# New states of the sample sequences: products over 32 rows, two sequences in different rows in turn, with four banks claimed at once

## The reference, cut to what matters

```python
s = (jnp.exp(b_last)[..., None] * s
     + jnp.einsum('bjhd,bjhv->bhdv', kc * jnp.exp(b_last[:, None] - b), vc))
```

## Time and profile before

| what | value |
|---|---|
| median of 3 runs | 1321.51 us |
| the profiled execution's own time | 1328.91 us |
| its span | 1327.0 us |
| TensorE busy | 1269.0 us (96%) |
| VectorE, ScalarE busy | 437.7 us (33%), 230.6 us (17%) |
| moved by DMA | 454.19 MB, mean 342 GB/s |
| mean granted TensorE clock | 0.983 of 2.4 GHz |

### The profile page before, as it was taken

The page is one execution under the profiler, slowest core; times in us unless marked ns, Lnnn a source line. Parts: engine busy times, 40 slices in busy tenths (PEclk is TensorE's granted clock), DMA queues, the critical chain, the costliest instruction groups (busy, mean ns, idle before and its releaser), DMA issues.

```text
span 1327.0 us, 16958 instructions
## 1 busy us (share of the span) xinstructions
PE 1269.0 (96%) x6497; PEld 702.9 (53%) x6497; DVE 437.7 (33%) x871; ACT 230.6 (17%) x360; POOL 29.3 (2%) x43
## 2 busy tenths in 40 slices
PE   6999999999899999999999999999999999999993
PEld 6999999987543434343443434343443434343431
DVE  4665565654322241313132231313132231313135
ACT  4633334410101011011101011011101011011112
POOL 0000010200000000000000000000000000000002
PEclk9999999999789999999999999999999999999997
DMA  9524444673589999999999999999999999999981
GB/s 379 193 106 143 162 155 157 262 292 127 198 332 377 418 416 417 417 418 417 417 417 416 416 418 418 417 418 417 417 417 416 417 416 418 417 418 417 417 337 41
DMA packets 81366, 454.19 MB, mean 342 GB/s; under 512 B 7437, under 2 KB 7565, under 8 KB 44456
## 3 DMA queue, kind: packets, MB, share of 16 engines
q1 hardware_dynamic: 77264, 439.63, 82.0%
q0 software_dynamic: 4064, 14.03, 3.1%
HBM read 447.44 MB, written 6.31 MB: 342 GB/s over the span
## 4 chain that ended last, share of the span: by engine, by line
PE 92%; DVE 4%; issue 2%; DMA 1%; ACT 0%; DVEq 0%; SPq 0%; ACTq 0%
PE bank L919 33%; PE bank L942 17%; PE bank L649 13%; PE bank L898 10%; PE bank L963 4%; PE bank L717 3%; PE bank L692 2%; PE bank L928 1%; PE bank L931 1%; PE bank L774 1%; PE bank L857 1%; DVE arena L1610 1%; DVE arena L1597 1%; PE bank L906 1%; PE bank L741 1%
## 5 line engine op out<-in xcount | busy, mean ns | idle before, releaser
L919 PE MATMUL bank<-ring,arena 128*64 128x512 f32 x1536 | 349.6, 595 | 0.0
L919 PEld LDWEIGHTS bank<-ring,arena 128*64 128x64 f32 x1536 | 119.5, 137 | 205.8 <-issue 205.8
L649 PE MATMUL bank<-arena_r,ring_r 128*128 128x320 f32 x848 | 182.8, 316 | 0.0
L942 PE MATMUL bank<-ring,arena 128*64 128x512 f32 x768 | 169.3, 593 | 1.3 <-ACT arena L1212 1.3
L1588 DVE TENSOR_TENSOR arena<-bank,arena 128x512 f32<-128x512 f32 x64 | 41.2, 686 | 359.5 <-PE bank L931 359.5
L649 PEld LDWEIGHTS bank<-arena_r,ring_r 128*128 128x128 f32 x848 | 138.7, 188 | 1.9 <-issue 1.8
L1581 DVE COPY arena<-bank 128x512 f32<-128x512 f32 x32 | 22.1, 692 | 327.8 <-PE bank L919 327.6
L898 PE MATMUL bank<-arena 128*128 128x128 f32 x720 | 127.9, 308 | 0.0
L919 PE MATMUL bank<-arena 128*64 128x512 f32 x512 | 119.4, 593 | 1.4 <-ACT arena L1194 1.4
L963 PE MATMUL bank<-arena 128*128 128x512 f32 (+1 forms) x192 | 93.0, 613 | 21.7 <-DVE arena L1610 15.9
L898 PEld LDWEIGHTS bank<-arena 128*128 128x128 f32 x720 | 97.9, 188 | 28.1
(11 more groups left out here) (213 smaller groups left out, 897.4 us busy)
## 6 DMA issues: line engine op xcount, KB each, us to landing
ring<-in_w_gu SPq DMA_DIRECT2D x192, 1024.0 KB, 14.9
ring<-in_w_down SPq DMA_DIRECT2D x96, 1024.0 KB, 17.8
arena<-in_w_gu SPq DMA_DIRECT2D x64, 1024.0 KB, 13.1
ring<-in_w_mix SPq DMA_DIRECT2D x32, 1024.0 KB, 5.1
arena<-in_w_down SPq DMA_DIRECT2D x32, 1024.0 KB, 16.5
arena<-in_state_gla POOLq DMA_DIRECT2D x4, 1024.0 KB, 10.3
out<-arena POOLq DMA_DIRECT2D x4, 1024.0 KB, 5.4
x_alone<-in_x_t SPq DMA_DIRECT2D x2, 640.0 KB, 4.6
```

The source lines that it names most:

```text
L649: last = mm(o[:, 0:NT], w[a][:, c, f0:f0 + 128], rhs[b][:, c, :], start=c == 0 and a + b == 0, stop=c == chunks - 1 and a == 1)
L919: last = mm(ex[i][side * CAP:(side + 1) * CAP, :], xgt[:, j, half * CAP:(half + 1) * CAP], w[:, i * D + side * 512:i * D + (side + 1) * 51 ...
L942: last = mm(ex[4][side * CAP:(side + 1) * CAP, :], actt[:, 2 * j + c, :], w[:, c, side * 512:(side + 1) * 512], start=j == 0 and c == 0, s ...
```

## The change

The product of sequence b now uses only 32 rows of the operands, those of the block of four sequences to which b belongs: rows 0 to 31 for sequences 0 to 3 (products 0 and 1), rows 32 to 63 for sequences 4 to 7 (products 2 and 3). The other rows held zeros for it. The calls now go in turn to a product in rows 0 to 31 and one in rows 32 to 63, which lie in different banks, and the order of the sequences is 0, 4, 1, 5, 2, 6, 3, 7. All four banks are claimed ahead of the first call.

```diff
                 pe.wait_ge(klm_ready, h + 1)
-                for i in range(4):
-                    o = claim(("kvs", h, i))
-                    for half in range(2):
-                        last = mm(o[:, half * DV:(half + 1) * DV], klm[:, 2 * i + half, :],
-                                  v[0:NS, 2, h * DV:(h + 1) * DV], start=True, stop=True)
-                    last.then_inc(full(("kvs", h, i))[0], 1)
+                held = [claim(("kvs", h, i)) for i in range(4)]
+                for half in range(2):
+                    for side in range(2):
+                        for g in range(2):
+                            i = 2 * g + half
+                            p0 = g * 32
+                            last = mm(held[i][:, side * DV:(side + 1) * DV], klm[p0:p0 + 32, 2 * i + side, :],
+                                      v[p0:p0 + 32, 2, h * DV:(h + 1) * DV], start=True, stop=True)
+                            if side == 1:
+                                last.then_inc(full(("kvs", h, i))[0], 1)
                 weights_times("ga", 2 * h, xt)
```

## The result

The changed kernel takes 1328.48 us in the median of 19 runs (1327.15 to 1333.86), the kernel before 1324.13 us in 19 runs taken beside it: ratio 1.0033, 95% interval 1.0018 to 1.0048. It is slower, by some 4.4 us.

What follows compares the result with a forecast made beforehand. TensorE was taken as the bound; per head 0.92 us of wait, -1.72 of overlap and +2.5 of clock fall gave +1.7, four heads +6.8, so 1321.5 + 6.8 = 1328.3 us, range 1317.0 to 1334.0.

Steps and rivals of the forecast that it cites:

- a step of +6.8: Four heads together: +1.7 us each, from -0.8 by instructions and +2.5 for a clock fall; from +2.4 to +9.2.
- a base of 1321.5: Whole kernel before: median 1321.51 us of the timed executions, to which the forecast step was added.
- What bounds: Whole kernel: TensorE bounds it, not weight transfers, so mixer time moves the expert part one for one.
- Overlap: Loop of each head: two 32-row groups run at once, 16 passes in 1.93 instead of 3.65 us, -1.72 a head.
- The wait: Ahead of each head's loop: TensorE idles 0.92 us until ScalarE's copy (L1122) frees the last claimed bank.
- -3.2 without the clock: Four heads, counted by instructions: 0.92 - 1.72 = -0.80 us each; as a rival 1318.3 us, chance 0.20.
- The clock falls in every head: Heads: clock drops to half between start of wait and end of loop, in all or nearly all heads; chance 0.64.
- Price of a fall: Each head: 2.5 us lost per clock fall, from 1.4 to 3.1.
- The part of `ga`: Gate product after the loop: 1.4 us lost per fall, as some 2.8 us of dense work run at half clock.
- the part of the loop: Each head's loop: 1.1 us lost per fall, two thirds of a possible 0 to 1.72.
- Displaced low stretches: Existing half-clock stretches near 325 and 366 us, shifted onto other work: counted 0, with 3 us on either side.
- the signs of being wrong: Included the half-clock stretches near 325 and 366 us vanishing or growing; no size given.

Runs made afterwards that it cites:

- wait-only: Kernel before with 64 rows and its old product order, only all four banks claimed ahead of the loop: 1344.92 us, 1.0131 of before.
- filled wait: The change with two dense 128-row products of constants run while TensorE would idle before the last bank: 1325.72 us, 0.9980 of before.
- between the gates: The change with its four-product loop moved between the head's two gate products: 1320.68 us, 0.9961 of before.
- wait in dense work: The change with each bank pair claimed just ahead of its products, plus an idle wait before each head's second gate product: 1321.59 us, 0.9994 of before.
- old order: Kernel before with products in order 0, 1, 2, 3 and banks claimed one by one, each product over only its 32 rows: 1326.48 us, 1.0005 of before.
- the same between the gates: 32-row loop moved between the two gate products, with products in order 0, 1, 2, 3 instead of the change's alternation: 1321.96 us, 0.9979 of before.
- late claim: The change with each pair of banks claimed just ahead of its products: 1317.22 us, 0.9936 of before.

## Why the prediction was right

It said 1328.3 us and slower; measured were 1328.48. Part of this closeness is luck: the forecast was a step of +6.8 on a base of 1321.5, and the step is +4.4 on 1324.1. Two errors of some 2.5 us, in the step and in the base, cancelled.

- *What bounds*: right. The 19.9 us of the wait-only heads show as 20.3 in the medians, and the experts' part stayed at 979.2 us in the first profile of the change. For the change itself the heads are longer by 4.86 us in one profile and by 6.43 in the other, and the medians differ by 4.35; as the levels of the router part mix into the medians, the closeness of 4.86 to 4.35 proves little.
- *Overlap*, -1.72 a head: right. 1.93 us were forecast, 1.93 measured at full clock (filled wait, between the gates), and 2.00 in the change's own head 0. Two passes start together at 100.1 us.
- *The wait*, 0.92 a head: 0.94 measured, released by the line that was named.
- *-3.2 without the clock*: the filled wait gives -3.25 in the heads.
- *The clock falls in every head*: right in both profiles of the change. That the emptiness of the wait does it is shown by the filled wait against the change, with nothing else altered but the dummy products, and by the wait alone. It didn't always fall within the stretch that was named: in heads 0 and 3 of the first profile it came down just after the loop.
- *Price of a fall*, 2.5 us: too high for the first profile, about right for the second. From the chain of the first, heads 0, 1 and 3 lost 1.59 us each, head 2 3.18 (loop plus `ga` over 1.93 + 7.25), 7.95 in all where 10 were forecast. The part of `ga` was taken too low (1.4; the four average 1.64) and the part of the loop too high (1.1; they average 0.35): in heads 0 and 3 the clock came down after the loop, in head 1 near its end, in head 2 in the midst of it. 4 x -0.80 + 7.95 = 4.75 is within 0.1 us of the heads' 4.86. In the second profile, with two low stretches of 6.83 us and two of 3.41, loop and `ga` lost 3.14, 3.18, 1.59 and 1.59, 9.50 in all; -3.2 + 9.50 = 6.3 is near its 6.43. Both the number and the length of the falls matter, and the length differs between executions of one kernel.
- *Displaced low stretches*, 0 with 3 us on either side: too small for a single execution. The router part differs by 5.4 us between the two profiles of the change, with 6.83 us of low clock at the router in one and 20.48 in the other, so this is not the shift's doing. That the stretch near 325 us would shrink stood among the signs of being wrong ("vanish or grow" in its words); it did shrink, in one profile of two. The base of 1321.5, from three runs, was one of its levels and the profiled execution another; the 7.4 us between them, which I carried over as a cost of profiling, is then mostly not one: executions of before outside a profile also take 1328.5 to 1329.6, at the same mean clock of 0.983 as the profiled one, and those near 1321.5 have 0.990.

The Trainium skill (TensorE: Matmul & The Clock Gate, A second HAM failure mode: psum-queue depth-cycling) says short idle times between groups of matmuls make the clock swing between its two levels. The wait-only run agrees (half clock in all heads from waits of 0.9 us); the wait in dense work shows that 0.60 us did nothing in the profiled execution, with full-height matmuls on both sides, and the old order shows falls with no idle time. The same page (Part 3: Packing small matmuls) has matmuls start strictly in program order. The runs in the old order differ: there 16 passes take 2.89 us instead of 3.65, since the second row group starts while passes ahead of it in the program are still to start.

Open: what the levels of before near 1321 and 1324 us look like inside. The mean clock (0.990 at 1321, 0.987 to 0.989 at 1324, 0.983 at 1329) says that they differ by time at half clock, but both profiles of before fell on the slowest level.

## What to carry to other kernels

Claim a bank where its first matmul stands, not at the head of a group: look up which product had it before, and when that product's reader ends. Before adding even a microsecond of idle time to TensorE, look whether its neighbours are thin (few rows, short passes); there the idle time is paid several times over in work that comes after it, and dense work inside it removed the price here. Whether dense work around it does is shown only for a shorter wait, in one profile. Where totals of one kernel spread by more than the effect, compare the same part of each profile.

## What was not expected of the hardware

- A wait of 0.9 us ahead of 3.65 us of 64-row passes cost 5 us a head, itself included: the clock was at half for 6.83 to 10.24 us each time (wait only).
- 32-row passes without any idle time were followed by a fall in all four heads (old order) or in two of four (the same between the gates), and 32-row passes in pairs by none (late claim).
- A second row group starts at once when four passes of the first stand ahead of it (L752), and after four when eight do (2.89 us for 16 passes, with or without a bank to wait for).
- The kernel before, unchanged, takes from 1321 to 1329 us. In both of its profiles the clock is at half for 20.48 us from 325 us on; where a profile has 6.83 to 13.65 us there, of the change for one, the same part is 5.0 to 5.5 us shorter.
